# Gate rows in the spent weight space beside the first head's products, and the down projection beside the last chunk's normalisation

## What is computed

```python
xm, o_pre = jnp.split(x @ w_in, 2, axis=-1)
xc = jax.nn.silu(_causal_dwconv(xm, conv_buf, conv_w, conv_b)[0])
q, k, v = _headwise(xc, w_q), _headwise(xc, w_k), _headwise(xm, w_v)
gates = jnp.concatenate([q, k, v], axis=-1) @ w_if + b_if
ig, lf = gates[..., :ML_HEADS], jax.nn.log_sigmoid(gates[..., ML_HEADS:])
h, C, n, m = _mlstm_cell(heads(q), heads(k) * ML_HEAD_DIM ** -0.5, heads(v), ig, lf, C, n, m)
hn = (h - mean(h)) * lax.rsqrt(var(h) + LN_EPS) * norm_g      # per head
return (sigmoid(o_pre) * (hn + skip * xc)) @ w_down, ...
```

## Time and profile before

| what | us |
|---|---|
| median of 3 runs (3279.12 to 3282.44) | 3281.55 |
| the profiled execution | 3282.95 |
| its span, first to last instruction | 3281.2 |
| TensorE busy | 3140.6 (96%) |
| VectorE busy | 1393.8 (42%) |
| ScalarE busy | 824.4 (25%) |
| GpSimd busy | 811.0 (25%) |

### The profile page before, as it was taken

How to read it: one execution, slowest core, us unless ns; L and a number is a source line. 1 busy time by engine, 2 the same in 40 slices (tenths; PEclk the granted TensorE clock), 3 DMA queues, 4 the chain that set the end, 5 groups by cost and what they waited for, 6 DMA issues and landing times.

```text
span 3281.2 us, 51779 instructions
## 1 busy us (share of the span) xinstructions
PE 3140.6 (96%) x20960; PEld 2899.5 (88%) x20960; DVE 1393.8 (42%) x2066; ACT 824.4 (25%) x1545; POOL 811.0 (25%) x520
## 2 busy tenths in 40 slices
PE   7999899999999999999979999998899999999997
PEld 7777689999999989999857777777898999999996
DVE  2000445333333354434338584857325433333335
ACT  4110523111111124111234444444105111111113
POOL 2112033333223232333101010101331333333320
PEclk9999899999999999999989999999999999999999
DMA  7454311111111113332235554637410111111111
GB/s 217 120 128 124 99 52 46 46 45 45 38 51 45 45 46 125 105 119 102 96 131 208 195 206 158 234 109 273 167 53 27 52 52 51 45 45 45 45 39 53
DMA packets 275662, 318.28 MB, mean 97 GB/s; under 512 B 23565, under 2 KB 215309, under 8 KB 274298
## 3 DMA queue, kind: packets, MB, share of 16 engines
q1 hardware_dynamic: 255265, 250.27, 24.7%
q10 hardware_dynamic: 12960, 40.04, 3.2%
q0 software_dynamic: 7296, 25.96, 2.3%
HBM read 224.88 MB, written 92.19 MB: 97 GB/s over the span
## 4 chain that ended last, share of the span: by engine, by line
PE 82%; DVE 8%; ACT 5%; issue 3%; DMA 1%; SPq 0%; POOL 0%; ACTq 0%; DVEq 0%; POOLq 0%
PE ps L373 23%; PE ps L374 22%; PE ps L375 22%; PE ps L1877 3%; PE ps L1089 1%; PE ps L1053 1%; PE ps L1033 1%; ACT X L456 1%; PE ps L1062 1%; DVE CT L1412 1%; PE ps L1063 1%; PE ps L1064 1%; PE ps L394 1%; PE ps L750 1%; ACT HT L1233 1%
## 5 line engine op out<-in xcount | busy, mean ns | idle before, releaser
L373 PE MATMUL ps<-AH,WH 128*128 128x352 f32 x3072 | 1000.2, 326 | 11.2 <-DVE AL L2346 6.3
L374 PE MATMUL ps<-AL,WH 128*128 128x352 f32 x3072 | 986.2, 321 | 0.0
L375 PE MATMUL ps<-AH,WL 128*128 128x352 f32 x3072 | 986.1, 321 | 0.0
L360 POOL TENSOR_SCALAR WH<-RAW 128x1024 fp32r<-128x1024 f32 x200 | 231.6, 1158 | 1730.4 <-PEq L380 1486.9
L373 PEld LDWEIGHTS ps<-AH,WH 128*128 128x128 f32 x3072 | 577.5, 188 | 36.9 <-issue 22.4
L374 PEld LDWEIGHTS ps<-AL,WH 128*128 128x128 f32 x3072 | 579.0, 188 | 1.0
L375 PEld LDWEIGHTS ps<-AH,WL 128*128 128x128 f32 x3072 | 577.3, 188 | 0.0
L362 POOL TENSOR_TENSOR WL<-RAW,WH 128x1024 fp32r<-128x1024 f32 x200 | 503.9, 2520 | 16.7
L373 PE MATMUL ps<-HH,WH 128*128 128x352 f32 x1536 | 498.4, 324 | 0.0
L374 PE MATMUL ps<-HL,WH 128*128 128x352 f32 x1536 | 492.3, 321 | 0.0
L375 PE MATMUL ps<-HH,WL 128*128 128x352 f32 x1536 | 492.0, 320 | 0.0
(11 more groups left out here) (291 smaller groups left out, 3517.3 us busy)
## 6 DMA issues: line engine op xcount, KB each, us to landing
RAW<-in_ffn_w SPq DMA_DIRECT2D x128, 512.0 KB, 3.8
CT<-in_state_mlstm_C SPq DMA_DIRECT2D x32, 1024.0 KB, 5.4
out_C_s<-CT SPq DMA_DIRECT2D x32, 1024.0 KB, 6.1
RAW<-in_ml_w_in SPq DMA_DIRECT2D x32, 512.0 KB, 3.9
RAW<-in_conv_w_pw SPq DMA_DIRECT2D x24, 512.0 KB, 8.9
STK<-u_scratch SPq DMA_DIRECT2D x48, 190.0 KB, 4.1
xc_scratch<-XC ACTq DMA_DIRECT2D x16, 528.0 KB, 2.7
so_scratch<-SO ACTq DMA_DIRECT2D x16, 528.0 KB, 3.6
```

Of the source, the lines that this page charges most:

```text
L360: pool.tensor_scalar(WH[:, k % 4], RAW[:, k % 2], 1.0, 0.0, ALU.mult, ALU.add).then_inc(w_hi, 1)
L373: pe.matmul(ps[:, bank, 0:CW], wh[:, k, cols], hi[:, k, cs], start=(k == 0), stop=False)
L374: pe.matmul(ps[:, bank, 0:CW], wh[:, k, cols], lo[:, k, cs], start=False, stop=False)
L375: mm = pe.matmul(ps[:, bank, 0:CW], wl[:, k, cols], hi[:, k, cs], start=False, stop=(k == nk - 1))
```

## The change

*Around the first head.* The gate rows and UM move to O_W, the space of RAW, WH and WL, which is free after phase A; FG and T1 lie over MT and BL. BD moves to the end of phase A's space, over SGX, V8 behind ROWB. So XCH and XMH of the first head are loaded at once when phase A's products have ended and its tiles 0 to 3 are in HBM; `block_weights(0)` stands ahead of the scans; the transposes of KM stand ahead of the last gate products, and ScalarE copies UM ahead of GE and issues the last tile's spills behind it. The query and key products wait only for the input gates' copy and their inputs. ScalarE does the 24 copies of them ahead of the last three exponentials (`row_exps`), TensorE turns CR (`row_columns`, bank 7) behind the ninth value product, VectorE does the value halves, then CC, then the terms of ROWB. GpSimd's first XO loads wait for the stored rows and t_cc.

*Around the last head.* DEC gets tiles of its own (HTD over QN, XOD0, XOD1) and bank 6 for its statistics. Panels 0 and 1 are loaded before the seventh memory of the last head is stored, ahead of WR, and split after the last low parts; panels 2 and 3 are loaded behind X. The variance product of END moves between the two products of the first (c, n) of the down projection. ScalarE copies END's raw output behind DEC's square and casts WR's chunks ahead of the roots and gains; VectorE subtracts each chunk ahead of the steps that follow. Every head now waits, before it writes QN, for the sample store of the head before.

The diff, cut to what the argument uses:

```diff
@@ -158,26 +160,27 @@
+        XMD = misc("XMD", [P, 2, NDEC])
         SGX = misc("SGX", [P, TOK])
-        XMD = misc("XMD", [P, 2, NDEC])
         RW = 2 * TOK + NDEC + NB
-        off[0] = O_A + VT * TOK * 4
-        IG = misc("IG", [HEADS, TOK])
-        FG = misc("FG", [HEADS, TOK])
...
+        off[0] = O_W
         MT = misc("MT", [HEADS, TOK])
         CR = misc("CR", [HEADS, TOK + NDEC])
+        IG = misc("IG", [HEADS, TOK])
+        LF = misc("LF", [HEADS, TOK])
+        O_BL = off[0]
+        BL = misc("BL", [HEADS, TOK])
...
+        UM = misc("UM", [MHIST * (1 + DEC_B), D_INNER])
...
+        FG = at("FG", [HEADS, TOK], F32, O_W)
+        T1 = at("T1", [HEADS, TOK], F32, O_BL)
+        assert off[0] <= O_M
...
+        V8 = misc("V8", [NDEC, DH])
+        off[0] = O_W - 3 * VT * P * 4
         BD = misc("BD", [P, 3, VT, P])
-        V8 = misc("V8", [NDEC, DH])
...
         DND = misc("DND", [P, NDEC])
         negd = misc("negd", [P, P])
+        HTD = at("HTD", [P, VT, NDEC], F32, off[0])
         QN = misc("QN", [P, VT, NDEC])
+        XOD0 = misc("XOD0", [P, VT, NDEC])
...
+        XOD1 = misc("XOD1", [P, VT, NDEC])
@@ def phase_b_sp @@
+                if last and b == 6:
+                    sp.wait_ge(hout, 5 * h + 2)
+                    for k in range(2):
+                        down_panel(sp, 0, k)
...
+        def ht(tc):
+            return HTD[:] if tc == DEC else HT[tc % 2][:, :, 0:TC[tc][1]]
+
+        def xo(tc, m):
+            return (XOD0, XOD1)[m][:] if tc == DEC else XO[tc % 2][:, m, :, 0:TC[tc][1]]
@@ def phase_b_pool @@
-            out_store(pool, h, DEC)
+            if h < HEADS - 1:
+                out_store(pool, h, DEC)
+
+        def stat_bank(tc):
+            return 6 if tc == DEC else 7
@@ def head_mean, head_var, row_columns @@
-            wait(pe, hsd, 5 * h + tc)
-            if tc == DEC:
-                pe.wait_ge(den_abs, 5 * h + END + 1)
+            if tc in (DEC, END):
+                pe.wait_ge(den_abs, 5 * h + tc + 1)
+            if tc != DEC:
+                wait(pe, hsd, 5 * h + min(tc, 3))
             pe.wait_ge(hsum, 10 * h + 2 * tc + 1)
-            pe.matmul(ps[:, 7, 0:w], ones_h[:], SQH[:, 0, 0:w], start=True, stop=True).then_inc(hmean, 1)
+            pe.matmul(ps[:, stat_bank(tc), 0:w], ones_h[:], SQH[:, 0, 0:w], start=True, stop=True).then_inc(hmean, 1)
...
-            pe.matmul(ps[:, 7, 256:256 + w], ones_h[:], SQH[:, 0, 0:w], start=True, stop=True).then_inc(hvar, 1)
+            pe.matmul(ps[:, stat_bank(tc), 256:256 + w], ones_h[:], SQH[:, 0, 0:w], start=True, stop=True).then_inc(hvar, 1)
+
+        def row_columns(pe):
+            pe.wait_ge(e_nrm, 1)
+            pe.wait_ge(gv, GV_END)
+            pe.wait_ge(ga_, GA_END)
+            for t in range(10):
+                m = P if t < 8 else NDEC
+                mm = pe.transpose(ps[0:m, 7, 4 * t:4 * t + 4], CR[:, t * P:t * P + m] if t < 9 else CR[:, TOK:TOK + NDEC], ident[0:4, 0:4])
+            mm.then_inc(t_cc, 1)
@@ def phase_b_pe @@
             if first:
                 pe.wait_ge(e_g, 2)
-                pe.wait_ge(e_nrm, 1)
-                pe.wait_ge(e_cc, 1)
...
+                if x == 9 and first:
+                    pe.wait_ge(e_cc, 1)
+                elif x == 9:
                     pe.wait_ge(hsd, 5 * h)
...
             for x in range(11):
+                if x == 0:
+                    wait(pe, hsd, 5 * h - 1)
                 if x == 1 or x == 2:
                     pe.wait_ge(qk_ev, 24 * h + 20 + x)
                 by_token(x)
+                if first and x == 8:
+                    row_columns(pe)
@@ def phase_b_act @@
             if first:
-                act.wait_ge(rs_out, 16)
-                act.wait_ge(d_out, 16 * 7)
+                act.wait_ge(e_g, 2)
...
             if first:
+                row_exps()
                 act.wait_ge(x_spill, 16)
+                act.wait_ge(spill[0], 16 * 4 * 8)
+                act.wait_ge(spill[1], 16 * 4 * 8)
...
+            if first:
+                act.wait_ge(rs_out, 16)
+                act.wait_ge(d_out, 16 * 7)
             act.wait_ge(bt_done, 8 * h + 8)
             act.activation(WS[:], BT[:, NB - 1], ACT.Exp, bias=ROWB[:, SEQ - 1:SEQ]).then_inc(ws_done, 1)
...
                 for tc in (0, 1, 2, END):
-                    if q == LAST[tc]:
+                    if q == LAST[tc] and not (tc == END and h == HEADS - 1):
                         raw_out(act, h, tc)
@@ def phase_b_dve @@
+                dve.wait_ge(spill[0], 16 * 4 * 8)
+                dve.wait_ge(spill[1], 16 * 4 * 8)
+                value_parts()
+                columns(dve)
+                dve.wait_ge(d_out, 16 * 7)
+                row_terms()
+            else:
+                row_terms()
+                value_parts()
...
             dve.wait_ge(e_nrm, 1)
+            wait(dve, o_out[1], 16 * 2 * h)
@@ block.sync @@
-            sp.wait_ge(spill[0], 16 * 4 * 8)
-            sp.wait_ge(spill[1], 16 * 4 * 8)
+            sp.wait_ge(spill[0], 16 * 4 * 2)
+            sp.wait_ge(spill[1], 16 * 4 * 2)
             sp.dma_start(XCH[:], inner_tiles(XCS, 0)).then_inc(ld_xc, 16)
+            sp.dma_start(XMH[:], inner_tiles(XMS, 0)).then_inc(ld_xm, 16)
...
-            sp.wait_ge(t_cc, 1)
-            sp.wait_ge(e_keep, 2 + 4)
-            sp.wait_ge(d_out, 16 * 7)
-            sp.dma_start(XMH[:], inner_tiles(XMS, 0)).then_inc(ld_xm, 16)
+            sp.wait_ge(spill[0], 16 * 4 * 8)
+            sp.wait_ge(spill[1], 16 * 4 * 8)
...
             sp.wait_ge(pv_mm, NS * HEADS - 3)
             x_back(0, 2)
-            sp.wait_ge(hout, 19)
...
-            down_panels(0)
+            sp.wait_ge(pv_mm, NS * HEADS)
+            sp.wait_ge(dec_mm, HEADS)
+            sp.wait_ge(dec_split, HEADS)
+            x_back(2, 5)
+            x_back(5, KT)
+            for k in range(2, 4):
+                down_panel(sp, 0, k)
@@ block.gpsimd @@
-            pool.wait_ge(w_free, NP_A + 32)
+            pool.wait_ge(rs_out, 16)
+            pool.wait_ge(d_out, 16 * 7)
+            pool.wait_ge(t_cc, 1)
             phase_b_pool(pool, 0)
             for h in range(1, HEADS):
                 phase_b_pool(pool, h)
-            pool.wait_ge(pv_mm, NS * HEADS)
+            pool.wait_ge(p_lo, NS * HEADS)
+            pool.wait_ge(upd_mm, 4 * DEC_B * HEADS)
+            split_panel(pool, NP_D, NP_D // 2 + 1, 0)
             pool.wait_ge(dexp, NS * HEADS)
-            pool.wait_ge(upd_mm, 4 * DEC_B * HEADS)
-            pool.wait_ge(o_out[1], 16 * 8)
-            for k in range(2):
-                split_panel(pool, NP_D + k, (NP_D + k) // 2 + 1, k)
+            pool.wait_ge(o_out[1], 16 * 7)
+            split_panel(pool, NP_D + 1, NP_D // 2 + 1, 1)
+            out_store(pool, HEADS - 1, DEC)
             out_store(pool, HEADS - 1, END)
             pool.wait_ge(o_out[0], 16 * 12)
             pool.wait_ge(hvar, 20)
@@ block.tensor @@
             free_panels(pe, ma_mm, 6 * NJ, 2)
-            gate_products(pe, NJ - 1, 1, last=True)
-
...
                 if j % 4 == 3:
                     mm.then_inc(t_keep, 1)
+            gate_products(pe, NJ - 1, 1, last=True)
             for m in (1, 0):
...
             pe.transpose(ps[:, 7, 0:P], NRW[:], ident[:]).then_inc(t_nrm, 1)
-            pe.wait_ge(gv, GV_END)
-            pe.wait_ge(ga_, GA_END)
...
             phase_b_pe(pe, 0, True)
...
             head_mean(pe, HEADS - 1, DEC)
             head_var(pe, HEADS - 1, DEC)
             head_mean(pe, HEADS - 1, END)
-            head_var(pe, HEADS - 1, END)
+            pe.wait_ge(num_ev, 5 * HEADS)
             pe.wait_ge(upd_ev, 4 * DEC_B * HEADS)
             pe.wait_ge(p_done, NS * HEADS)
             for c in range(3):
-                down(c, 0, c, lambda h: 2 * c + h)
+                down(c, 0, c, lambda h: 2 * c + h, None if c else lambda c, u: head_var(pe, HEADS - 1, END))
@@ block.scalar @@
             gate_sigmoid(act, NJ - 1, 1)
-            spill_tile(act, NJ - 1, 1)
+            act.wait_ge(ma_mm, 6 * NJ)
+            for q in range(4):
+                act.wait_ge(t_keep, 2 + q + 1)
+                act.copy(UM[:, 512 * q:512 * q + 512], ps[0:27, q, :]).then_inc(e_keep, 1)
             act.wait_ge(gate_mm, NJ)
             for g, (lo, w) in enumerate(GCOLS):
                 p = slice(32 * g, 32 * g + 8)
                 act.activation(GE[p, 0:w], ps[p, 6, 0:w], ACT.Identity, bias=BIFC[p]).then_inc(ge_ev, 1)
-            for q in range(4):
-                act.wait_ge(t_keep, 2 + q + 1)
-                act.copy(UM[:, 512 * q:512 * q + 512], ps[0:27, q, :]).then_inc(e_keep, 1)
+            spill_tile(act, NJ - 1, 1)
 
...
             act.copy(NT[:].rearrange("p b j -> p (b j)"), ps[:, 7, 0:P]).then_inc(e_nrm, 1)
-            act.wait_ge(gv, GV_ROWS)
-            alink(act.activation(RP[:, TOK:2 * TOK], MT[:], ACT.Exp, scale=-2.0))
...
+            def row_exps():
+                act.wait_ge(gv, GV_ROWS)
...
```

(30 more changed lines are left out.)

128 lines of the change are left out of this document (58 added, 70 removed).

## The result

| what | us |
|---|---|
| median before (4 runs, 3279.12 to 3282.44) | 3281.35 |
| median after (4 runs, 3256.49 to 3259.83) | 3258.35 |
| ratio, with its 95% interval | 0.9931 (0.9918 to 0.9943) |
| profiled execution after, its span | 3259.83, 3258.1 |
| the same after kernel in a later comparison (5 runs against 9 of before) | 3259.4 against 3280.05 |

The change saves 23.0 us in the first comparison and 20.7 in the second. I had forecast 16.3: the direction was right, the median is 0.65 us under my range. The experiments ask where the other 4 to 7 us are.

The account below looks back on a forecast made before the run. TensorE, busy 96% of the span, was taken as the bound, so only its idle or half-clock time could be won. Savings of 9.3 + 7.0 = 16.3 took 3282.95 to 3266.7, less 1.4 for the median: 3265.3, range 3262 to 3269.

Parts of the forecast that it names:

- Place one: Start of the first head, around the gate rows: 9.3 us saved, bounds 4.5 and 13.5.
- the walk to the prompt memory: First head, from ScalarE's copies near 1647.9 to the prompt memory at 1681.8: it starts 11.4 us earlier.
- The 24 copies: ScalarE's query and key copies in the first head: 0.58 us each, 13.9 in all, ending at 1661.8.
- The half clock right behind the pause: Prompt memory, after TensorE idles some 5 us: some four microseconds at half rate, about 2.1 us given back.
- The heads between keep their order, apart from waits that are long met: Between the first head's start and the last head's end: nothing else on TensorE's path, no cost.
- Place two: After the last head: down projection starts 8.0 us earlier, less 1.0 for a stall; 7.0 saved, bounds 2.5 and 10.3.
- the lock's price: After the last head: GpSimd's panel splits and VectorE's small operations block each other; 2.3 us, bounds 0 and 3.1.
- The second pair of panels: Down projection: panels 2 and 3, split late, make TensorE stall; 1.0 us subtracted, a wait of 0 to 2 expected.
- The spills' issue: ScalarE's four DMA issues near GE: costed at nothing; as rival, slow issues lose the whole gain, 3282.3, chance 0.02.
- a late store of the last chunk: Rival: store lands late beside full queues, TensorE waits at the second pair of panels; total 11.8, 3270, chance 0.15.
- a late ROWB: Rival, first head: ROWB issued 4.8 us later and landing 11.9 after; total saving 11.5, 3270, chance 0.13.
- Both pauses vanish: Rival: no lock, full clock, quick ROWB; 13 + 10 = 23 us saved, 3259, chance 0.12.

Follow-up runs that it names:

- one: The kernel before with only the change around the gate rows and first head, tail left as before: 3267.31 us against 3279.08, ratio 0.9965.
- again: The changed kernel run once more, unchanged, against the kernel before: 3259.40 us against 3280.05.
- pad: The changed kernel with 30 filling products on TensorE ahead of the prompt memory: 3268.50 us (one run).
- lock: The changed kernel with GpSimd's splits of the first two panels held until the second sum of the sample columns: 3263.75 us (one run), against 3280.32 before.

## Why the prediction was too small

- **Place one, the walk to the prompt memory: right in its steps, three terms too long.** Measured from XC, I put the prompt memory 50.5 behind it (1681.8 less 1631.3); it came 44.8, 44.8 and 46.4 behind. Term by term, in the trace of after: ScalarE's copies started 2.4 earlier (14.2 behind XC, not 16.6). GE no longer stands behind the four spill issues and starts 2.75 behind XC, not 4.25; UM's copies no longer stand between GE and the regrouping (TensorE waited 1.6 for them before), and from GE to IG go 4.1 and not 4.9. I had cost that reordering at nothing. The 24 copies took 11.9 and not 13.9: 0.58 is the pace at which TensorE makes products, and six were already waiting when ScalarE began, so the first twelve took 4.82. From the exponentials' end to ROWB's issue went 2.6 and not 4.0: I took the value near the old row, but nearly half of the old row's 4.8 was something else than the row table's landing (small stores, XMH on the queue). ROWB took 0.3 less than 7.9. BT to the prompt memory took 5.6 and not 5.2. The sum is 5.7.
- **The half clock right behind the pause: right**, 1.5 instead of 2.1, with a pause of 3.8 instead of 5.
- **A term that was missing.** "The heads between keep their order, apart from waits that are long met": the order is kept, the clock is not. From the prompt memory to the head copy the kernels with place one lost 3.4 (`one`), 3.2 (`again`) and 6.6 (after), 1.5 of it right behind the pause and the rest at the heads' ends, where the kernels without an unfilled pause lose no more than before did (see `pad`). With the three terms and the cheaper clock alone, place one would be worth 17.1 - 1.5 = 15.6; by the times it is 11.8, so some 3.8 were taken back. 9.3 was forecast, and the interval of the run reaches from 7 to 15.
- **Place two: right in its mechanism, the lock's price too high.** The first down product comes 9.8 earlier behind the head copy (22.9 before, 13.1 after), forecast 8.0. The hold that I expected is there (0.88, 2.27 and 1.76 for three operations), but the first two were over at 2272.89, before TensorE came to the product of the mean at 2273.81 (4.6 behind the head copy, as before and in `lock`), so the centre did not move, and of the third only 0.7 reached the path, as a later subtraction of WR (2278.88, where its cast had ended at 2278.18). I charged the full 2.3, the length of one hold in the earlier trace rows, and did not ask what slack stood behind it. The remaining 0.2 are gaps that I had rounded up.
- **The second pair of panels: right in kind**, one wait of 0.4, forecast 1.0. Behind the start of the projection 1.5 are given back in the mean: this 0.4; 0.5 for END's variance product, which now stands between the first two products (from the 21st to the 41st matmul go 3.6 us, 3.1 before); the rest in gaps of tenths. The half clock there is not what costs: over the first 40 us it takes 2.0 to 2.3 without place two and 2.0 to 2.6 with it, in the six traces of the table. Net 8.9 by the stretches, 7.9 by the run, forecast 7.0.
- **The spills' issue**: 0.35 to 0.50 each, beside the copies of GE, nothing. **Rivals**: neither a late store of the last chunk (the split that waits for it starts 3.3 behind its issue, 3.4 before) nor a late ROWB (issued at 1659, its four loads landed 7.3 to 8.4 behind their issue) came. "Both pauses vanish" gives the right number, 3259, for a wrong reason: one pause of 3.8 stayed and with it the half clock.
- **What is luck.** In the first pair of traces 3.8 us lie ahead of any changed instruction, and the median of before was 3281.35, 3279.08 and 3280.05 in three comparisons. The sum of the parts (19.7) and the second comparison (20.7) are nearer to what the change does, 3.4 to 4.4 above my forecast. It is luck too that place one (11.8) lies within my bounds of 4.5 to 13.5: the walk alone gained 17.1, and the half clock that I had left out took some of it back.

The step that failed is thus the sizing of place one. I put the prompt memory 11.4 earlier, and it came 17.1 earlier: the start of ScalarE's copies, costed at nothing, gave 2.4, the 24 copies took 2.0 less, the issue of ROWB came 1.4 sooner behind the exponentials. I had read these terms from rows that held the pace or the work of others, and had given bounds to the ROWB terms only, so that the walk passed its own upper bound (11.4 + 1.5 + 0.3 = 13.2; the 13.5 of the prediction is 0.3 more than its terms add up to). And I let the range end at the rival's number, 3259, and not at the sum of the upper bounds (13.2 + 10.3, or 3258.1), which is just under the 3258.35 measured.

## What to carry to other kernels

A duration read from a row belongs to whoever set the pace there: ask for each term of a walk which engine would set it after the change. A step that is held up costs what reaches the path behind it, not its own length. When a row table feeds one product, give its chain (here BT, WS, WK, WKL) VectorE first and the steps that nobody waits for after it: with the row table made earlier that was worth 9.6 here, more than half of place one. And price a new pause of TensorE by a run in which it is filled: here it cost more than the half clock right behind it.
